# Rider products in blocks of three weight rows instead of two, in an expert layer that streams its weights

## The chip, the cores and the metric

One core of a Trainium2 chip runs the kernel. The metric is the device time of one execution, in microseconds (us). Three timed runs of the kernel before gave 2209.34, 2218.16 and 2219.35 us; the median is 2218.16. The profiled execution took 2214.47 us.

## The reference

One inference step of a two-layer encoder for 512 prompt tokens and 128 sample tokens (640 together), model width 1024, all in float32. Layer 0 ends in a dense SwiGLU, layer 1 in a mixture of eight experts with two per token. Only the experts matter here:

```
logits = x @ w_router + b_router; top_v, top_i = top_k(logits, 2); gates = softmax(top_v)
y = sum over e of comb[:, e] * ((silu(x @ we1[e]) * (x @ we3[e])) @ we2[e])
```

`we1[e]` and `we3[e]` are 1024 x 1408, `we2[e]` is 1408 x 1024.

## The kernel before

**Passes.** The expert layer runs in eleven passes, each with one expert's weights. A pass takes 128 tokens; in the first five (the "ridden" ones) 32 more tokens, the riders, go through the same weights. The up half of a pass multiplies by `we1` and `we3`, the down half by `we2`. The halves are staggered: up of pass 0, up of pass 1, down of pass 0, up of pass 2, down of pass 1 and so on. Three rounds of "down, then up" of ridden passes run in a loop; then come a ridden down, an up without riders, the last ridden down, and plain passes to the end.

**Weight rows.** Weights come as rows of 128 partitions: 16 up rows of 1408 columns (704 KB), called U0 to U15 here, and 11 down rows of 1024 columns (512 KB), D0 to D10. They go through a ring of nine places (`NPLACE`, line 76). SyncE issues one DMA per row (line 671) as soon as the place of the row nine earlier is free. The first TensorE instruction after a row's products and after what rides behind them frees the place: `free_place` (line 1575) lets it add one to `expert_used`.

**What happens to a row.** ScalarE makes a rounded copy ("upper", line 2303), VectorE subtracts it from the raw row and writes the rest ("lower", line 3192) over the raw row, in place. TensorE multiplies the 128 tokens by both parts: nine matmuls for an up row, six for a down row. The riders instead are multiplied by the raw row, in full float32, by `ride` (line 1632): four matmuls in four column groups of 32, each run as two passes. A ride waits until its row's DMA has landed (`expert_in`), and VectorE's subtraction waits for the ride (`rows_ridden`, line 3199), since it overwrites what the ride reads.

**Order on TensorE.** It is written out by hand and executed in order. With `LOOK` = 5, after the products of every second row c, TensorE rides rows c+5 and c+6. I call such a group of rides a block. In the up half blocks follow c = 1, 3, ..., 15; in the down half they follow f = 0, 2, ..., 10, and rows beyond D10 are the next half's U0 to U5. Between rows TensorE also turns (transposes) gathered tokens and products (`turn_rows`, `turn_riders`, `turn_product`, `turn_rider_product`).

**Other traffic.** GpSimd gathers the next tokens from HBM early in each down half and stores a pass's result, 512 KB and four times 32 KB, at the end of each down half, beside the weight rows.

Of the kernel before, what the change touches and what calls it, by code (L numbers as in the profile page):

```python
# [85 lines left out]
LOOK = 5  # L86
# [112 lines left out]
def build(nc, a, c, o, d):  # L199
# [11 lines left out]
    with ctx:  # L211
# [701 lines left out]
        def _(pe):  # L913
# [5 lines left out]
            def wait(s, value):  # L919
                pe.wait_ge(s, value)  # L920
# [4 lines left out]
            def claim(*banks):  # L925
                for b in banks:
                    if holder[b]:
                        wait(*holder[b])
                        holder[b] = None
# [17 lines left out]
            def product(out, x, y, first, last):  # L947

                ins = mm(out, x[0], y[0], first, False)
                mm(out, x[0], y[1], False, False)  # L950
                return ins, mm(out, x[1], y[0], False, last)
# [143 lines left out]
            for l in range(DEPTH):  # L1095
# [470 lines left out]
                if l % 2:  # L1566
# [8 lines left out]
                    def free_place(ins):  # L1575

                        if release[0]:
                            ins.then_inc(expert_used, 1)
                            release[0] = False

                    def weight_parts():

                        nonlocal place
                        take(expert_split)
                        at = place % NPLACE
                        place += 1
                        return expert_upper(at), ERL[:, at, :]

                    def turn_rows(half, bank):

                        if half == 0:
                            take(gathered_in, 16)
                        claim(bank)
                        for j in range(4):
                            ins = tr(PS[:, bank, tiles(j)], GR[:, tiles(4 * half + j)])
                            free_place(ins)
                        ins.then_inc(rows_turned, 1)
                        holder[bank] = (rows_split, n.add("rows_split"))
# [33 lines left out]
                    def ride(row, up_row=None, down_row=None):  # L1632

                        at = row % NPLACE
                        landed = 16 * (row // NPLACE + 1)
                        wait(expert_in[at], landed if riders.i is None else riders.i * (16 * PASS_ROWS // NPLACE) + landed)
                        if down_row is None:
                            k, which = UP_ORDER[up_row]
                            b, width, starts, first, last = 3 + 4 * which, RIDER_COLS, RIDER_AT, k == 0, k == KD - 1
                            stationary = [XR[:, k, :]] * 4  # L1640
                            if up_row == 0:
                                wait(riders_ready, riders.value("riders_ready"))
                        else:
                            b, width, starts, first, last = 2, D // 4, range(0, D, D // 4), down_row == 0, down_row == NF - 1
                            group, j = RIDER_BLOCK[down_row]
                            stationary = [ACTR[:, j, RIDERS * group:RIDERS * (group + 1)]] * 4
                            if down_row == 0:
                                wait(rider_product_ready, riders.value("rider_product_ready"))
                        if first:
                            claim(b)  # L1650
                        for g in range(4):
                            ins = mm(PS[RIDERS * g:RIDERS * (g + 1), b, 0:width], stationary[g],
                                     ER[:, at, starts[g]:starts[g] + width], first, last)
                        ins.then_inc(rows_ridden, 1)
                        if last:
                            made = {2: rider_y_ready, 3: rider_silu_made, 7: rider_product_made}[b]
                            holder[b] = (made, riders.add(made.name))

                    def up(ridden, following):

                        wait(rows_split, n.value("rows_split"))
                        for c in range(UP_ROWS):
                            k, which = UP_ORDER[c]
                            w = weight_parts()
                            for part in PART_ORDER:
                                first, end = PARTS[part]
                                b = 4 * which + part
                                if k == 0:
                                    claim(b)
                                begin, ins = product(PS[:, b, 0:end - first], [x[:, k, :] for x in (XGH, XGL)],  # L1670
                                                     [x[:, first:end] for x in w], k == 0, k == KD - 1)
                                free_place(begin)
                                if k == KD - 1:
                                    ins.then_inc((gates_summed, ups_summed)[which], 1)
                                    made = (silu_made, product_made)[which]
                                    holder[b] = (made, n.add(made.name))
                            release[0] = True
                            for ahead in range(c + LOOK, c + LOOK + 2) if c % 2 else ():
                                if ridden and ahead < UP_ROWS:
                                    ride(place - 1 + ahead - c, up_row=ahead)  # L1680
                                if following and UP_ROWS <= ahead < UP_ROWS + LOOK:
                                    ride(place - 1 + ahead - c, down_row=ahead - UP_ROWS)
                            if c == 13:
                                turn_rows(0, 0)

                    def down(ridden, rows, products):

                        banks = (0, 1) if ridden else (3, 7)
                        for f in range(NF):
                            w = weight_parts()  # L1690
                            if f == 0:
                                wait(product_split, n.value("product_split"))
                            for half, b in enumerate(banks):
                                if f == 0:
                                    claim(b)
                                begin, ins = product(PS[:, b, :], [x[:, f, :] for x in (ACTH, ACTL)],
                                                     [x[:, half * 512:(half + 1) * 512] for x in w], f == 0, f == NF - 1)
                                free_place(begin)
                                if f == NF - 1:
                                    ins.then_inc(down_summed, 1)  # L1700
                                    holder[b] = (moe_y_ready, n.add("moe_y_ready"))
                            release[0] = True
                            for ahead in range(f + LOOK, f + LOOK + 2) if f % 2 == 0 else ():
                                if ridden and ahead < NF:
                                    ride(place - 1 + ahead - f, down_row=ahead)
                                if rows == "ridden" and ahead >= NF:
                                    ride(place - 1 + ahead - f, up_row=ahead - NF)
                            if rows and f == 0:
                                turn_rows(1, 7 if ridden else 0)
                            if rows == "ridden" and f == 1:  # L1710
                                turn_riders(3)
                            if products and f in (4, 8):
                                turn_product(f // 4 - 1)
                            if products == "ridden" and f == 9:
                                turn_rider_product()
                        if products:
                            turn_product(2)
# [18 lines left out]
                    for c in range(LOOK + 1):  # L1736
                        ride(c, up_row=c)
                    up(True, False)
                    turn_rows(1, 1)
                    turn_riders(3)  # L1740
# [75 lines left out]
                for it in range(4):  # L1816
# [35 lines left out]
                    for j, blocks in enumerate(W2_CHUNKS):  # L1852
                        c = len(UP_CHUNKS) + j
# [1582 lines left out]
```

## Time and profile before

| | us |
|---|---|
| timed runs, median of 3 | 2218.16 (2209.34 to 2219.35) |
| profiled execution | 2214.47 |
| its span, first to last instruction | 2212.8 |
| expert layer, first row issued to last (DMA table) | 1496.7 to 2160.0 |
| rides, first to last | 1520.0 to 1905.4 |
| TensorE busy in the span | 2042.4 (92%) |
| VectorE busy | 1307.5 (59%) |
| ScalarE busy | 997.3 (45%) |

In the rows further down the first number is a start in us from the span's start, the next a duration; the text in square brackets is the time for which the engine was idle before, and what ended it. PE is TensorE, DVE VectorE, ACT ScalarE, POOL GpSimd, SPq the SyncE queue. All matmuls of the layer have line 941, since a helper records them; they are told apart by their tiles: `expert_ring,mix_t` is a ride of an up or down row (384 or 256 columns), `region_split`, `expert_lower` and `z_weights_upper` are products with the split rows. Lines 1889 and 2524 are the helpers of ScalarE and VectorE.

### The profile page before, as it was taken

The numbers are of one execution on the slowest core, as the hardware profiler recorded it, in microseconds if no ns is written. First come the engines' busy times: TensorE is split into PE (matmuls) and PEld (weight loads), VectorE is DVE, ScalarE is ACT, GpSimd is POOL, SyncE is SP. The second block draws the span as 40 slices with busy tenths as digits, with TensorE's granted clock in tenths as the row PEclk, the third lists the DMA queues.
The fourth block names the chain that finished last, engine by engine and source line by source line (L and its number), as shares of the span: only waits on it lengthen the run. The fifth ranks groups of instructions, "written<-read, shape, count | busy, mean of one in ns | idle before, by whom it ended". The sixth has DMA issues, their size and how long they took to land.

```text
span 2212.8 us, 36684 instructions
## 1 busy us (share of the span) xinstructions
PE 2042.4 (92%) x14292; PEld 1713.2 (77%) x14292; DVE 1307.5 (59%) x2052; ACT 997.3 (45%) x1456; POOL 185.1 (8%) x271
## 2 busy tenths in 40 slices
PE   6999868898999999998999788978999999999996
PEld 4999645588999999998998445866666667788883
DVE  3657654355544544456567643645566667789885
ACT  5422126444424433434221254434455556677782
POOL 3000120110000000000000011111010010011201
PEclk8999769998999999999998689978999999999998
DMA  9222669633545454642123266216677788899995
GB/s 319 77 77 77 164 185 300 206 103 96 169 127 167 129 159 127 166 146 78 60 77 86 58 222 207 83 61 228 224 260 248 256 279 324 323 372 375 371 385 190
DMA packets 272094, 418.23 MB, mean 189 GB/s; under 512 B 21214, under 2 KB 216312, under 8 KB 271952
## 3 DMA queue, kind: packets, MB, share of 16 engines
q1 hardware_dynamic: 249984, 349.50, 47.8%
q0 software_dynamic: 21968, 66.72, 9.2%
q8 instruction: 102, 1.67, 0.3%
q14 instruction: 40, 0.33, 0.0%
HBM read 385.73 MB, written 29.59 MB: 188 GB/s over the span
## 4 chain that ended last, share of the span: by engine, by line
PE 81%; DMA 6%; DVE 5%; ACT 3%; issue 2%; SPq 1%; ACTq 0%; POOL 0%; PEldq 0%; DVEq 0%; PEld 0%; POOLq 0%
PE banks L941 78%; PE banks L945 3%; DMA expert_ring<-in_we 2%; DMA weight_ring<-in_w_ada 2%; DVE scratch L2524 1%; ACT scratch L1889 1%; DVE region L2524 1%; ACT hidden_t L1889 1%; DMA scratch<-bias_rows 1%; SPq L588 1%; ACT region_split L1889 1%; ACTq L1904 0%; DMA mix_t<-h_rows,pass_tokens 0%; DMA weight_ring<-in_w_in 0%; DVE weights_lower L2524 0%
## 5 line engine op out<-in xcount | busy, mean ns | idle before, releaser
L941 PE MATMUL banks<-upper_parts,region_split 128*128 128x320 f32 x1664 | 390.5, 310 | 4.5 <-DVE upper_parts L2524 4.5
L941 PE MATMUL banks<-upper_parts,weights_lower 128*128 128x320 f32 (+1 forms) x1248 | 387.2, 310 | 0.0
L941 PE MATMUL banks<-region_split 128*128 128x320 f32 (+1 forms) x1264 | 338.9, 331 | 2.5 <-DVE upper_parts L2524 2.5
L2524 DVE TENSOR_TENSOR expert_lower<-expert_ring,region_split 128x1408 fp32r<-128x1408 f32 (+1 forms) x198 | 284.1, 1468 | 93.3 <-PE banks L941 64.0
L941 PEld LDWEIGHTS banks<-upper_parts,region_split 128*128 128x128 f32 x1664 | 284.9, 189 | 4.8 <-issue 4.8
L1889 ACT ACTIVATE region_split<-expert_ring 128x1408 fp32r<-128x1408 f32 (+1 forms) x198 | 242.3, 1256 | 68.8 <-DMA expert_ring<-in_we 56.4
L941 PEld LDWEIGHTS banks<-region_split 128*128 128x128 f32 x1264 | 222.9, 188 | 19.0 <-issue 4.8
L941 PEld LDWEIGHTS banks<-upper_parts,weights_lower 128*128 128x128 f32 (+1 forms) x1248 | 235.4, 189 | 0.0
L941 PE MATMUL banks<-region_split,upper_parts 128*128 128x384 f32 x732 | 226.5, 379 | 0.0
L2524 DVE TENSOR_TENSOR weights_lower<-weight_ring,region_split 128x2048 fp32r<-128x2048 f32 (+2 forms) x72 | 168.9, 2350 | 96.3 <-ACT region_split L1889 96.2
L1889 ACT ACTIVATE region_split<-weight_ring 128x2048 fp32r<-128x2048 f32 (+2 forms) x72 | 140.6, 1958 | 164.1 <-PE banks L941 162.5
L1889 ACT ACTIVATE region<-banks 128x320 f32<-128x320 f32 (+4 forms) x178 | 78.6, 461 | 267.4 <-PE banks L941 264.2
L941 PE MATMUL banks<-expert_lower,upper_parts 128*128 128x384 f32 x528 | 198.0, 375 | 0.0
L941 PE MATMUL banks<-z_weights_upper,upper_parts 128*128 128x256 f32 (+2 forms) x644 | 193.9, 335 | 0.6 <-ACT hidden_t L1889 0.5
L941 PE MATMUL banks<-region_split,weights_lower 128*128 128x320 f32 x608 | 187.9, 309 | 0.0
L2524 DVE TENSOR_TENSOR expert_lower<-expert_ring,z_weights_upper 128x1408 fp32r<-128x1408 f32 (+1 forms) x99 | 141.8, 1441 | 71.3 <-PE banks L941 45.6
L941 PE MATMUL banks<-upper_parts,z_weights_upper 128*128 128x320 f32 (+1 forms) x544 | 171.0, 314 | 11.7 <-DVE hidden_lower_parts L2524 10.2
L941 PE MATMUL banks<-hidden_lower_parts,z_weights_upper 128*128 128x320 f32 (+1 forms) x544 | 170.0, 313 | 0.0
L941 PEld LDWEIGHTS banks<-region_split,upper_parts 128*128 128x128 f32 x732 | 135.9, 188 | 32.1 <-issue 12.1
L1889 ACT ACTIVATE z_weights_upper<-expert_ring 128x1408 fp32r<-128x1408 f32 (+1 forms) x99 | 121.8, 1234 | 65.5 <-DMA expert_ring<-in_we 65.5
L941 PEld LDWEIGHTS banks<-z_weights_upper,upper_parts 128*128 128x128 f32 x644 | 120.9, 189 | 17.7 <-issue 7.6
L941 PEld LDWEIGHTS banks<-upper_parts,z_weights_upper 128*128 128x128 f32 (+1 forms) x544 | 102.9, 189 | 18.0 <-issue 15.6
(333 smaller groups left out, 3265.6 us busy)
## 6 DMA issues: line engine op xcount, KB each, us to landing
expert_ring<-in_we SPq DMA_DIRECT2D x176, 704.0 KB, 6.7
expert_ring<-in_we SPq DMA_DIRECT2D x121, 512.0 KB, 4.4
weight_ring<-in_w_ada SPq DMA_DIRECT2D x48, 1024.0 KB, 9.3
weight_ring<-in_w SPq DMA_DIRECT2D x88, 512.0 KB, 4.8
weight_ring<-in_w_in SPq DMA_DIRECT2D x24, 1024.0 KB, 5.2
weight_ring<-in_w SPq DMA_DIRECT2D x16, 1408.0 KB, 6.3
weight_ring<-in_w_out SPq DMA_DIRECT2D x8, 1024.0 KB, 7.0
y_rows<-residual_t POOLq DMA_DIRECT2D x4, 1760.0 KB, 23.6
```

Of the source, the lines that this page charges most:

```text
L588: sp.dma_start(dst, src).then_inc(weights_in[q % NSLOT], 16)
L941: return nc.tensor.matmul(out, lhsT, rhs, start=first, stop=last)
L945: return nc.tensor.transpose(out, in_, ident[0:k, 0:k])
L1889: return nc.scalar.activation(out, in_, f, **kw)
L2524: return v.tensor_tensor(out, x, y, op)
```

## The change

The blocks of rides become larger and rarer: three rows after every third row. In the up half they follow c = 1, 4, 7, 10, 13 and ride c+5, c+6 and c+7; in the down half they follow f = 0, 3, 6, 9 and ride f+5, f+6 and f+7. The same rides are made with the same operands; products, turns, frees and DMAs keep their order among themselves.

```
-                            for ahead in range(c + LOOK, c + LOOK + 2) if c % 2 else ():
+                            for ahead in range(c + LOOK, c + LOOK + 3) if c % 3 == 1 else ():
                                 if ridden and ahead < UP_ROWS:
                                     ride(place - 1 + ahead - c, up_row=ahead)
...
-                            for ahead in range(f + LOOK, f + LOOK + 2) if f % 2 == 0 else ():
+                            for ahead in range(f + LOOK, f + LOOK + 3) if f % 3 == 0 else ():
                                 if ridden and ahead < NF:
                                     ride(place - 1 + ahead - f, down_row=ahead)
```

## Rows read from the trace of the kernel before

**Rows 1.** The page: the span, and the chain that ended last by line
```profile
span 2212.8 us, 36684 instructions
...
PE banks L941 78%; PE banks L945 3%; DMA expert_ring<-in_we 2%; DMA weight_ring<-in_w_ada 2%; DVE scratch L2524 1%; ACT scratch L1889 1%; DVE region L2524 1%; ACT hidden_t L1889 1%; DMA scratch<-bias_rows 1%; SPq L588 1%; ACT region_split L1889 1%; ACTq L1904 0%; DMA mix_t<-h_rows,pass_tokens 0%; DMA weight_ring<-in_w_in 0%; DVE weights_lower L2524 0%
```
**Rows 2.** Busy time by stretch: ridden, then plain; last columns clock, DMA share, GB/s
```profile
1650.00:1700.00 50.00, 50.00 (x329) 33.85 (x328) 31.89 (x27) 27.72 (x28) 2.65 (x5) 1.00 0.76 256
...
2050.00:2100.00 50.00, 50.00 (x241) 42.45 (x240) 44.71 (x38) 39.24 (x40) 10.30 (x5) 1.00 0.97 380
```
**Rows 3.** PE in order of time: blocks after U1 and U3, first product between
```profile
1656.38 1.50 PE L941 MATMUL banks<-expert_ring,mix_t 128*32 128x384 f32 x16
1657.81 0.44 PE L941 MATMUL banks<-region_split,upper_parts 128*128 128x384 f32 x1
...
1661.84 1.50 PE L941 MATMUL banks<-expert_ring,mix_t 128*32 128x384 f32 x16
```
**Rows 4.** PE in order of time: blocks after D2 and D4 of the fourth down
```profile
1842.86 1.07 PE L941 MATMUL banks<-expert_ring,mix_t 128*32 128x256 f32 x16
...
1846.85 0.64 PE L941 MATMUL banks<-expert_ring,mix_t 128*32 128x256 f32 x8
1847.98 0.64 PE L941 MATMUL banks<-expert_ring,mix_t 128*32 128x256 f32 x8 [0.49 <-DMA expert_ring<-in_we]
```
**Rows 5.** Issues by SP: a U10, then U5, U8, U11, a later U8, a D10
```profile
1587.68 0.33 SPq L671 DMA_DIRECT2D expert_ring<-in_we  x1
...
1644.61 0.33 SPq L671 DMA_DIRECT2D expert_ring<-in_we  x1
...
1652.41 0.33 SPq L671 DMA_DIRECT2D expert_ring<-in_we  x1
...
1660.20 0.33 SPq L671 DMA_DIRECT2D expert_ring<-in_we  x1
...
1794.63 0.33 SPq L671 DMA_DIRECT2D expert_ring<-in_we  x1
...
1841.95 0.33 SPq L671 DMA_DIRECT2D expert_ring<-in_we  x1
```
**Rows 6.** ACT taking rows as they land: U10, then U2, U8, U11, a later U8
```profile
1591.67 1.38 ACT L1889 ACTIVATE z_weights_upper<-expert_ring 128x1408 fp32r<-128x1408 f32 x1 [1.94 <-DMA expert_ring<-in_we]
...
1643.49 1.39 ACT L1889 ACTIVATE region_split<-expert_ring 128x1408 fp32r<-128x1408 f32 x1 [0.35 <-DMA expert_ring<-in_we]
...
1660.00 1.38 ACT L1889 ACTIVATE z_weights_upper<-expert_ring 128x1408 fp32r<-128x1408 f32 x1 [3.21 <-DMA expert_ring<-in_we]
...
1665.42 1.38 ACT L1889 ACTIVATE region_split<-expert_ring 128x1408 fp32r<-128x1408 f32 x1 [0.43 <-DMA expert_ring<-in_we]
...
1801.46 1.38 ACT L1889 ACTIVATE z_weights_upper<-expert_ring 128x1408 fp32r<-128x1408 f32 x1 [2.46 <-DMA expert_ring<-in_we]
```
**Rows 7.** POOL: the store of a pass's result after D10
```profile
1652.05 0.60 POOL L854 DMA_DIRECT2D y_rows<-hidden_t  x1 [17.11 <-ACT hidden_t L1889]
```
**Rows 8.** PE: the block after D6, rides of U0 and U1
```profile
1640.45 0.85 PE L941 MATMUL banks<-expert_ring,mix_t 128*32 128x384 f32 x8
1641.78 0.85 PE L941 MATMUL banks<-expert_ring,mix_t 128*32 128x384 f32 x8 [0.48 <-DMA expert_ring<-in_we]
```
**Rows 9.** DMA issues of 1644.5 to 1644.8, U5: KB, us to landing
```profile
expert_ring<-in_we SPq DMA_DIRECT2D x1, 704.0 KB, 6.0
```
**Rows 10.** PE: second products of U10 and U11 (no riders), block after U11
```profile
1878.54 0.34 PE L941 MATMUL banks<-expert_lower,upper_parts 128*128 128x384 f32 x1
...
1880.45 0.34 PE L941 MATMUL banks<-expert_lower,upper_parts 128*128 128x384 f32 x1
...
1882.47 0.64 PE L941 MATMUL banks<-expert_ring,mix_t 128*32 128x256 f32 x8
1883.64 0.64 PE L941 MATMUL banks<-expert_ring,mix_t 128*32 128x256 f32 x8 [0.53 <-DMA expert_ring<-in_we]
```
**Rows 11.** PE: the longest wait in the ridden stretch
```profile
1578.53 2.48 PE L945 MATMUL banks<-ident,region 128*128 128x128 f32 x14 [3.88 <-DVE region L2524]
```
**Rows 12.** Busy time in the stretch behind that wait
```profile
1580.00:1585.00 5.00, 5.00 (x21) 4.45 (x20) 3.74 (x5) 4.83 (x6) 0.00 (x0) 0.69 0.01 3
```

More of the change, by code:

```diff
@@ L1677, in up @@
                             release[0] = True
-                            for ahead in range(c + LOOK, c + LOOK + 2) if c % 2 else ():
+                            for ahead in range(c + LOOK, c + LOOK + 3) if c % 3 == 1 else ():
                                 if ridden and ahead < UP_ROWS:
@@ L1702, in down @@
                             release[0] = True
-                            for ahead in range(f + LOOK, f + LOOK + 2) if f % 2 == 0 else ():
+                            for ahead in range(f + LOOK, f + LOOK + 3) if f % 3 == 0 else ():
                                 if ridden and ahead < NF:
```

## Prediction, written before the changed kernel had run

> **What bounds the kernel now.** I read the page first: four fifths of the chain that ended last are TensorE's own matmuls, 78% on line 941 [rows 1]. So in the expert layer nearly all that TensorE does or waits for moves the end. The view by stretches shows the same from another side: in the ridden stretch TensorE has work for all of 50 us, VectorE is busy for 31.9 us and the DMA share is 0.76; in the plain stretch the DMA share is 0.97 at 380 GB/s, but TensorE is again never idle [rows 2]. What a ridden pass loses is therefore not given back later. The clock is 1.00 in both, its 2.4 GHz level.
>
> Then I went through TensorE in order of time, for what a block costs, and through SyncE's issues and ScalarE's waits, for when rows land. ScalarE takes a row at once when it has been waiting for it, so its start is the landing time within some 0.03 us.
>
> **What the change removes: entries into blocks.** A ride leaves 8 records, and the first ride of a block, 8 records, ends 0.85 us after it began [rows 8]; two rides, 16 records, end after 1.50 [rows 3]. So a further up ride adds 0.65 us. For down rides it is 0.64 and 1.07, thus 0.43 [rows 4]. From one pair block to the next, with two up rows between, are 1661.84 - 1656.38 = 5.46 us [rows 3]. A row without a block takes 1880.45 - 1878.54 = 1.91 us [rows 10]. That leaves 5.46 - 2 x 1.91 - 2 x 0.65 = 0.34 us for entering and leaving a block; part of it is seen in the first product behind it, 0.44 us long [rows 3] where 0.33 to 0.34 is usual [rows 10]. In the down half the pair period is 1846.85 - 1842.86 = 3.99 [rows 4]; a down row, 6 matmuls of 512 columns against an up row's 4224 columns, is then 1.91 x 3072 / 4224 = 1.39, and the entry 3.99 - 2.78 - 0.86 = 0.35.
>
> The rides stay 135 in number, 12 of them ahead of the first two ups. Counted out from the code, blocks before: 5 and 8 in the first two ups, 6 + 8 in each of three loop rounds, 3 + 3 in the next down and up, 3 in the last ridden down: 64. After: 4 and 5, then 3 x (4 + 5), 2 + 2, 2: 42. The 22 entries saved give 22 x 0.34 = 7.5 us.
>
> **What it moves: each third row is ridden a row earlier.** This is the costly part. Row c+7 goes into the place of row c-2, which is freed when row c-1 begins. In the pair order row c+6 was the last of a block, freed one row sooner. So the time from freeing to riding the last row of a block falls by a whole row, to the rows c-1 and c, 3.82 us, and two rides, 1.3 us. From the DMA's issue, 0.37 to 0.5 us after the freeing, to the start of the third ride it is 2 x 1.91 - 0.37 + 0.10 + 0.35 + 3 x 0.32 = 4.9 us for an up row. TensorE executes in order: behind a ride that waits stand the next row's products, behind these the next frees, so SyncE's next issues and VectorE's subtractions come later too. Nothing of TensorE's can pass it, and the whole wait counts. Now each block:
>
> - U8, in the block after U1 (three loop rounds). It is issued at 1652.41, when TensorE turns the last product part, just after D10 [rows 5], at the very time at which the pass's result starts to be stored [rows 7]. It lands at 1660.00 [rows 6], 7.6 us later; now it is ridden only after U3. In the new block its ride could start at 1656.38 + 0.35 + 3 x 0.32 = 1657.7 [rows 3]: a wait of 2.4 us with the 0.09 us that PE takes after a landing. In the third round U8 takes 1801.46 - 1794.63 = 6.8 us [rows 5, 6]: a wait of 1.6. Taken: 3 x 2.0 = 5.9. Bounds: 0 and 7.5.
> - U11 and U14, in the blocks after U4 and U7 (five ups, ten cases). U11 was issued at 1660.20 and landed at 1665.42 [rows 5, 6], 5.2 us; wanted at 4.9, so a wait of 0.4. The least that a 704 KB row takes is 1591.67 - 1587.68 = 4.0 [rows 5, 6], no wait; a second row of a group tends to the slow side. Taken 0.35: 10 x 0.35 = 3.5. Bounds: 0 and 9, the latter at the 6 us of U5 [rows 9] less a little.
> - U5, in the block after D9 (three). Issued at D8's start, wanted after the rest of D8, the turn of a product part (0.4), D9 and two rides, some 4.1 us later. It takes 6.0 us now [rows 9] and 4.0 at the least: a wait of 0 to 2.0. With fewer DMAs ahead of it in the new order: 1.2, three times 3.6.
> - U1 and U2, in the block after D6 (three). Here TensorE waits already: U1's ride starts at 1641.78 where 1641.1 was possible, 0.7 us [rows 8]. U2, now ridden two rows later, lands at 1643.49 [rows 6] and is wanted at 1641.8: a wait of 1.7, which contains the old one. U0 and U2 are issued up to 1.4 and 1.0 us earlier in the new order, but two entries fewer bring the block nearer too. Additional wait -0.3 to 1.8, taken 0.8: 2.4.
> - D10, in the block after D3 (in the two downs that no ridden up follows). Issued at 1841.95 [rows 5], it lands so late that TensorE waits even after D4: from 1847.3 to 1847.98 [rows 4]. In the new order it is wanted at 1842.75 + 1.39 + 0.10 + 0.26 + 0.65 = 1845.2. The wait is 2.8 instead of 0.65, 2.2 more; two of them 4.4. With the low end, half of it, the gather that slows it would have to be over earlier.
> - D0 and D1, in the block after U10 of the up without riders. D0's ride starts at 1882.47 and D1's at 1883.64, the latter waiting [rows 10]; the new block would stand ready at 1880.45 - 0.17 + 0.10 = 1880.4 and can't be done before 1883.9. U11, 1.9 us, then comes behind it instead of before: 2.0 more.
> - Other blocks find their rows landed (D4 in the block after U13, D7 after D0, all rows of the first block): nothing.
>
> VectorE gets three rows to subtract at once, one after another; it has 18 us of 50 to spare in this stretch [rows 2], and the first row of a block is multiplied only four rows after it. That hides the bunching. Were that cover gone, a subtraction late would cost 1 to 2 us per block, some 40 to 80 us.
>
> Sum: 5.9 + 3.5 + 3.6 + 2.4 + 4.4 + 2.0 = 21.8 us of waits, less 7.5 us: 14.3 us more. On the profiled execution's 2214.5 that gives 2228.8; the median shown lies 3.7 us above it, so the forecast for a median is 2218.2 + 14.3 = 2232.5 us.
>
> A rule of the Trainium skill speaks for the change. "DMA: Bandwidth & Descriptors", in "Anatomy of one DMA", puts a DMA's time (fitted on GpSimd's path) at about 2.0 us plus bytes over 436 GB/s: for 720,896 bytes an estimate of 3.65 us. The trace does not agree where it matters: 4.0 at the least, 5.2 to 7.6 beside other transfers [rows 5, 6, 9]. By the rule all waits but those of D0 and D1 would be gone; it is the third rival below.
>
> **The rivals.**
> - The waits relieve each other (0.24). While TensorE waits it frees no places, so the DMA queues empty and the next row lands faster. Then U8 costs as above, but U11, U14, U5 and U2 next to nothing: 5.9 + 4.4 + 2.0 + 9.5 / 10 = 13.2, and if U8 too loses half of its wait, 10.3. Less 7.5 this is 3 to 6 us more, 2221 to 2224. For it: the DMA share of only 0.76 [rows 2] and 4.0 us for a row issued into calm [rows 5, 6]. Against it: U8's lateness has the result's store beside it [rows 7], which no wait of TensorE moves away.
> - On the other side (0.10): rows land in time because load sets the landing, and the new order spreads it. One mechanism: at the 4.0 us of the quiet U10 [rows 5, 6] a row beats each of the distances 4.1 (U5), 4.9 (U11, U14) and 5.3 (U8). It decides from the point at which U8 lands within 5.3 us of its issue. Then only the 22 entries are left, -7.5 us, 2210.7; with D0 and D1 still late 2212.7. Rows of 5.2 to 7.6 us speak against it. By the page's 3.65 us it would come out at the same 2210.7 to 2212.7.
> - The waits cost the clock (0.06). After TensorE had waited 3.88 us [rows 11] the next 5 us were granted 0.69 [rows 12], which is partly the 1.2 GHz level. The waits here are up to 2.8 us (D10) and 2.4 us (U8). If each of these five dropped the clock as there, (1 - 0.69) x 5 = 1.6 us each, 8 us would come on top: 2240. Against it: the waits of 0.5 to 1 us in the ridden stretch are followed by no drop [rows 2].
>
> **How the numbers follow.** Forecast 0.60, the others 0.24, 0.10 and 0.06. A measurement of this kernel can tell about 0.5%, 11 us, from no change: under 2207 counts as faster, over 2229 as slower. The forecast's own range is 2225 to 2240. The whole range begins at 2212, where the waits just pay for themselves less the scatter of the runs, and ends at 2245, with the upper bounds 7.5, 9, 6, 5.4, 4.4 and 2.0 (34.3 less 7.5 is 26.8 more). Slower: 0.62, from the forecast without its lower edge and from the clock case. Within: 0.33, from that edge, the first rival and most of the second. Faster: 0.05, half of the second rival.
>
> **What would show it.** TensorE's waits for `expert_ring` DMAs between 1520 and 1905 should rise from about 3 us to over 20, the largest behind U1, D3 and, once, U10; U8's ride should start right after ScalarE's start on U8. The pair period of 5.46 us should become 3 x 1.91 + 6 rides' passes of 0.32 + 0.34 = 8.0 us for three rows where nothing waits. The plain stretch should be as long as before. I am wrong if U8 lands within 5.3 us of its issue, if a block's entry costs far more or less than 0.34 us, or if VectorE's subtractions become what products wait for.

## The result, and the profile after

| | before | after |
|---|---|---|
| median (lowest to highest) | 2218.22 us (2209.34 to 2219.35), 6 runs | 2241.45 us (2234.45 to 2244.41), 6 runs |
| ratio | | 1.0103, 95% interval 1.0087 to 1.0119 |
| profiled execution | 2214.47 | 2243.98 |
| first to last issue of an expert row | 1496.7 to 2160.0: 663.3 us | 1502.7 to 2189.4: 686.7 us |

The kernel is 23 us slower. In the profiled executions 6.0 of the 29.5 us of difference lie before the first expert row, in code that did not change; over the executions profiled for this case that start lies anywhere from 1496.0 to 1503.3. So I compare the length of the expert layer, issue to issue: 23.4 us longer. One run of e11, an experiment below, took 6708.4 us, three times as long as any other; it is left out of every figure here.

The page after, span and chain; against [rows 1] TensorE's share of the chain falls from 78% to 76% and that of the expert rows' DMAs rises from 2% to 5%:

```profile
span 2242.3 us, 36684 instructions
...
PE banks L941 76%; DMA expert_ring<-in_we 5%; PE banks L945 4%; DVE scratch L2524 1%; ACT scratch L1889 1%; DVE region L2524 1%; ACT hidden_t L1889 1%; DMA scratch<-bias_rows 1%; ACT region_split L1889 1%; ACT region L1889 0%; ACTq L1904 0%
```

TensorE's waits for expert rows (total us, times, longest), before, then after:

```profile
PE banks L941 <- DMA expert_ring<-in_we: 3.6, 7, 0.7
```
```profile
PE banks L941 <- DMA expert_ring<-in_we: 24.4, 20, 4.9
```

Busy time by stretch, after (the columns are those of [rows 2]: length, busy time of TensorE, its weight loads, VectorE, ScalarE and GpSimd, then clock, DMA share and GB/s). The first two lines are the ridden stretch, the last the plain one [rows 2]. In the ridden stretch TensorE now idles and the clock is no longer 1.00; the plain stretch is as it was.

```profile
1600.00:1650.00 50.00, 48.11 (x332) 32.71 (x330) 30.05 (x27) 24.49 (x27) 2.37 (x4) 1.00 0.75 243
1650.00:1700.00 50.00, 46.45 (x285) 31.91 (x285) 27.84 (x22) 26.51 (x27) 2.65 (x5) 0.97 0.73 243
...
2050.00:2100.00 50.00, 50.00 (x241) 42.46 (x240) 43.73 (x37) 38.54 (x38) 3.81 (x4) 1.00 0.98 382
```

TensorE in order of time, after, from the block behind D9 to the block behind U7 of the first loop round; x24 is the number of records in a group, 8 for each ride:

```profile
1656.11 1.50 PE L941 MATMUL banks<-expert_ring,mix_t 128*32 128x384 f32 x16
1659.60 0.85 PE L941 MATMUL banks<-expert_ring,mix_t 128*32 128x384 f32 x8 [1.99 <-DMA expert_ring<-in_we]
1660.38 0.90 PE L945 MATMUL banks<-ident,region 128*128 128x128 f32 x3
1660.93 0.78 PE L941 MATMUL banks<-z_weights_upper,region_split 128*128 128x512 f32 x1
1661.51 0.63 PE L941 MATMUL banks<-expert_lower,region_split 128*128 128x512 f32 x1
...
1667.97 2.14 PE L941 MATMUL banks<-expert_ring,mix_t 128*32 128x384 f32 x24
1670.04 0.45 PE L941 MATMUL banks<-region_split,upper_parts 128*128 128x384 f32 x1
...
1675.98 1.50 PE L941 MATMUL banks<-expert_ring,mix_t 128*32 128x384 f32 x16
1678.33 0.85 PE L941 MATMUL banks<-expert_ring,mix_t 128*32 128x384 f32 x8 [0.84 <-DMA expert_ring<-in_we]
...
1685.04 0.53 PE L941 MATMUL banks<-expert_ring,mix_t 128*32 128x384 f32 x4
```

Three things are to be seen. Where the third row has landed, a block is one group of 24 records in 2.14 us (behind U1: no wait for U8 here). Where it has not, the group breaks into 16 and 8 with the wait between: 2.0 us for U5, 0.8 us for U11. And behind the wait for U5 a matmul of 512 columns takes 0.63 us instead of 0.39: part of D10's products ran at the 1.2 GHz level. From the block at 1675.98 to the next are 9.06 us; less the wait that is 8.0 to 8.2, where [rows 3] had 5.46 for two rows.

The granted clock around the three places in the ridden part where this happened, and at a fourth near the layer's end (second number from the end but one):

```profile
1660.00:1665.00 5.00, 5.00 (x25) 3.90 (x18) 0.00 (x0) 2.21 (x4) 0.00 (x0) 0.66 0.42 149
...
1900.00:1910.00 10.00, 8.96 (x51) 6.62 (x55) 4.91 (x4) 3.57 (x4) 0.00 (x0) 0.83 0.55 173
1928.00:1938.00 10.00, 8.91 (x38) 6.67 (x39) 3.29 (x3) 4.21 (x5) 0.00 (x0) 0.73 0.61 190
...
2184.00:2194.00 10.00, 9.44 (x34) 7.64 (x35) 7.32 (x7) 5.86 (x7) 0.54 (x1) 0.83 0.67 232
```

Not every such wait was followed by a fall. Around the wait for U5 of the third loop round (2.17 us, until 1808.34) and around the first of the waits for D10 shown below (2.30 us, until 1865.83) the clock stayed at 1.00:

```profile
1806.00:1816.00 10.00, 7.83 (x54) 5.49 (x54) 4.30 (x3) 6.00 (x8) 2.64 (x5) 1.00 0.75 266
1864.00:1874.00 10.00, 8.17 (x44) 6.39 (x45) 6.11 (x7) 4.33 (x5) 0.00 (x0) 1.00 0.83 289
```

And the two waits for D10 in the block behind D3, after (for before, see [rows 4]):

```profile
1865.83 0.64 PE L941 MATMUL banks<-expert_ring,mix_t 128*32 128x256 f32 x8 [2.30 <-DMA expert_ring<-in_we]
...
1929.09 1.08 PE L941 MATMUL banks<-expert_ring,mix_t 128*32 128x256 f32 x8 [4.90 <-DMA expert_ring<-in_we]
```

### The profile page after: what moved, and what is told of

Its sections match the earlier page's. It is cut to its first block, busy times and chain, and to the rows that moved or that the text cites. A ratio compares the mean times of both kernels' runs of the same rounds, so it can differ in the third digit from the quotient of the medians.

```text
span 2242.3 us, 36684 instructions
## 1 busy us (share of the span) xinstructions
PE 2051.8 (92%) x14292; PEld 1723.7 (77%) x14292; DVE 1305.9 (58%) x2052; ACT 996.3 (44%) x1456; POOL 175.6 (8%) x271
## 3 DMA queue, kind: packets, MB, share of 16 engines
q8 instruction: 102, 1.67, 0.3%
## 4 chain that ended last, share of the span: by engine, by line
PE 80%; DMA 8%; DVE 5%; ACT 4%; issue 2%; ACTq 0%; POOL 0%; PEldq 0%; DVEq 0%; PEld 0%; POOLq 0%; SPq 0%
PE banks L941 76%; DMA expert_ring<-in_we 5%; PE banks L945 4%; DVE scratch L2524 1%; ACT scratch L1889 1%; DVE region L2524 1%; ACT hidden_t L1889 1%; DMA scratch<-bias_rows 1%; ACT region_split L1889 1%; ACT region L1889 0%; ACTq L1904 0%; DVE weights_lower L2524 0%; DMA hidden_t<-h_rows,pass_tokens 0%; DMA weight_ring<-in_w_ada 0%; ACT L1889 0%
```

## The experiments

Theory A is the prediction's: the last row of a block of three is ridden one row sooner after its place is freed, and TensorE waits for its landing. Theory B, a rival: three rides in a row cost by themselves, because VectorE gets its rows in bunches. Theory C, the prediction's last rival made a second cause: the waits lower the clock. "Layer" is first to last issue of an expert row in the profiled execution, against 663.3 us before. "PE waits for rows" is TensorE's time in waits for rows from 1536 to 1935, and how often. All ratios are against the kernel before on the same chip: its median was 2216.8 us beside e1 to e4, 2217.1 beside e5 to e8 and 2217.6 beside e9 to e12.

| label | blocks | LOOK | median | ratio (95%) | layer | PE waits for rows |
|---|---|---|---|---|---|---|
| before | 2 and 2 | 5 | 2218.2 | 1 | 663.3 | 3.6 us, 7 times |
| after | 3 and 3 | 5 | 2241.5 | 1.0103 (1.0087 to 1.0119) | +23.4 | 24.4, 20 |
| e1 | up 3, down 2 | 5 | 2234.5 | 1.0082 (1.0052 to 1.0112) | +16.9 | 17.5, 15 |
| e2 | up 2, down 3 | 5 | 2235.3 | 1.0067 (1.0039 to 1.0095) | +18.4 | 17.0, 12 |
| e3 | 3 and 3 | 4 | 2209.0 | 0.9969 (0.9950 to 0.9988) | -7.7 | 1.8, 2 |
| e4 | 2 and 2 | 4 | 2215.0 | 0.9987 (0.9971 to 1.0002) | -1.6 | none |
| e5 | 4 and 4 | 3 | 2205.9 | 0.9940 (0.9918 to 0.9962) | -10.0 | 1.8, 3 |
| e6 | 3 and 3 | 3 | 2206.6 | 0.9940 (0.9921 to 0.9959) | -10.5 | none |
| e7 | 1 and 1 | 5 | 2237.0 | 1.0084 (1.0059 to 1.0109) | +17.9 | 2.8, 3 |
| e8 | e1 with filling | 5 | 2229.0 | 1.0056 (1.0035 to 1.0077) | +11.6 | 10.1, 16 |
| e9 | e6 again | 3 | 2209.2 | 0.9953 (0.9936 to 0.9970) | -9.0 | none |
| e10 | e5 again | 3 | 2207.0 | 0.9954 (0.9937 to 0.9970) | -10.7 | 1.4, 1 |
| e11 | e1 again | 5 | 2231.0 | 1.0060 (1.0040 to 1.0080) | +11.2 | 16.2, 19 |
| e12 | e8 again | 5 | 2228.2 | 1.0049 (1.0031 to 1.0067) | +15.2 | 11.5, 14 |

**e1 and e2: each half of the change alone.** e1 takes only the line of the up half from the change, e2 only that of the down half.

> Blocks of three in the up halves only, pairs in the down halves. Theory A (the last row of a block is ridden one row sooner after its place is freed, and TensorE waits for its landing): 14 entries less, -4.8 us; U8 is again issued beside the result's store and late, since no wait for U5 stands ahead of it: 3 x 2.0; U11 and U14 0.2 to 1.0 each as in the changed kernel, together about 4.5; D0 and D1 2.0. Sum about +7 to +8 us, ratio 1.003 to 1.004. Theory B (three rides in a row cost by themselves, by bunching VectorE's subtractions): the loss of 21 us goes by blocks, 14 of 22 of it: +13 us. Theory C (the clock falls after long waits): no fall here, as no wait reaches 3 us.

> Blocks of three in the down halves only. Theory A: 8 entries less, -2.8 us; waits for U2 (1.0 more in each loop round), U5 (1.7 to 2.4 in each), D7 about 0.8 once, D10 2.2 and about 4.4: together +15, sum about +12 us, ratio 1.0055. Theory B: 8 of 22 of 21 us, +8 us. Theory C: D10's product after the wait for U5 runs at half clock in at least one round, 1 us each, within the +12.

Both halves lose, and both more than expected: +18 us for +7 to +8 in e1, +15 to +18 for +12 in e2. Their sum is more than the whole change (layers +16.9 and +18.4 against +23.4, ratios +0.82% and +0.67% against +1.03%), so they share something. A part of it is U8. TensorE in e1, the block behind U1 of the first loop round, the product behind it, and ScalarE's take of the same row:

```profile
1656.99 1.50 PE L941 MATMUL banks<-expert_ring,mix_t 128*32 128x384 f32 x16
1660.92 1.30 PE L941 MATMUL banks<-expert_ring,mix_t 128*32 128x384 f32 x8 [2.44 <-DMA expert_ring<-in_we]
1662.15 0.69 PE L941 MATMUL banks<-region_split,upper_parts 128*128 128x384 f32 x1
```
```profile
1660.90 1.38 ACT L1889 ACTIVATE z_weights_upper<-expert_ring 128x1408 fp32r<-128x1408 f32 x1 [3.52 <-DMA expert_ring<-in_we]
```

The ride starts within 0.02 us of ScalarE's take of the same row: it is the landing that ends the wait. From where the third ride could start (1656.99 + 0.35 + 3 x 0.32 = 1658.3) it is 2.6 us, and the other two rounds have 2.6 and 2.45: 7.7 us for U8 where the prediction had 5.9, and where the whole change has 2.3. There the wait for U5 stands just ahead, the DMA share is down to 0.42 when U8 is issued (the row 1660.00:1665.00 above), and in round one U8 lands in time (the unbroken group at 1667.97 above). e1 was expected at +7 to +8 and came at +18 (its repeat e11 at +13): theory A's sum fell short. Besides the larger waits for U8, and one of 2.55 us for the last D10 though e1's down halves are unchanged, the clock was missing from it. The matmul at 0.69 us shows it, and so does the clock in the stretches behind the three waits for U8, 0.91 over 20 us each, 1.8 us of clock apiece:

```profile
1600.00:1660.00 60.00, 57.71 (x392) 38.99 (x390) 36.93 (x34) 32.10 (x36) 5.85 (x9) 1.00 0.79 265
1660.00:1680.00 20.00, 18.31 (x110) 12.13 (x110) 9.23 (x7) 10.64 (x11) 0.00 (x0) 0.91 0.66 223
1735.00:1755.00 20.00, 18.44 (x111) 12.06 (x112) 9.40 (x7) 10.16 (x11) 0.00 (x0) 0.91 0.68 228
1810.00:1830.00 20.00, 19.37 (x115) 13.50 (x116) 9.43 (x7) 10.97 (x11) 0.00 (x0) 0.91 0.65 220
```

So the expectation of no fall in e1, since no wait reaches 3 us, was wrong. In e2 the clock fell behind two of the three waits for U5 (1.96 and 2.11 us) and both for D10 (3.36 and 3.56 us), 0.83 over the 10 us around each.

Theory B would have e1 lose nearly twice what e2 does, by blocks; they lose the same within their intervals. Taken alone, e1's loss is nearer to B's +13 us than to A's +7 to +8, and e11's +13 is B's figure. So these two runs don't decide; the next does.

**e3 and e4: the same blocks, ridden later after the freeing.**

```
-LOOK = 5
+LOOK = 4
```

(e3: with both lines of the change; e4: with pairs.)

> The change with LOOK = 4: after every third row the rows c+4, c+5 and c+6 are ridden, so the last row of a block has the same distance from its freeing as in the kernel before, and the first rows are ridden a row later than there. Theory A: the added waits go, the 22 entries stay saved: -7.5 us against before, or a little better where the old waits for U1, D0, D1 and D10 shrink; ratio 0.996 to 0.997. Theory B: still 21 us slower than before, or more, as VectorE has one row less between ride and product; ratio 1.01.

> The kernel before with LOOK = 4: pairs of rows c+4 and c+5. The last row of a block is ridden a row later after its freeing than before. Theory A: the old waits of TensorE on expert rows, about 4.5 us, mostly go, entries stay: -3 to -4 us, ratio 0.998; against it the three-row kernel with LOOK = 4 is 3 to 5 us faster. Theory B: no different from before, unless VectorE becomes late, then slower.

This decides between A and B. e3 has exactly the changed kernel's blocks and makes it some 30 us faster than the change (0.9969 against 1.0103), and faster than before with an interval clear of 1, as theory A gave it. By theory B it had to stay slow. TensorE in e3, three blocks of the first up in the loop, all unbroken:

```profile
1656.55 2.14 PE L941 MATMUL banks<-expert_ring,mix_t 128*32 128x384 f32 x24
...
1664.56 2.14 PE L941 MATMUL banks<-expert_ring,mix_t 128*32 128x384 f32 x24
...
1672.59 2.14 PE L941 MATMUL banks<-expert_ring,mix_t 128*32 128x384 f32 x24
```

e4 removes the old waits and gains at most a little: its interval touches 1. (In its profiled execution, as in those of e9 and after, the layer's last stretch ran at 0.83 over 10 us behind a wait for VectorE, which costs it as much as 2 us of layer.)

**e5 and e6, and again as e10 and e9: LOOK = 3.** e5 rides four rows after every fourth (`range(c + LOOK, c + LOOK + 4) if c % 4 == 1`, and `f % 4 == 0`), e6 is the change with LOOK = 3.

> LOOK = 3 and blocks of four, after every fourth row: rows c+3 to c+6. The last row of a block keeps the distance of the kernel before, and there are 33 blocks instead of 64: 31 entries saved, -10.5 us. Theory A: about 10 us faster than before, 3 us faster than three rows with LOOK = 4, ratio 0.995. Theory B (bunching makes VectorE late): the first row of a block has only two rows between ride and product, 3.8 us for a landing on VectorE of 1.6 us, but D3 is now ridden only after the next half begins, and VectorE's multiplications wait for it; if that shows, the gain is smaller than 7 us or a loss.

> LOOK = 3 and blocks of three: rows c+3 to c+5, the last row one row later after its freeing than before. Theory A: entries -7.5 us, the old waits on expert rows (4.5 us) gone: -11 to -12 us, ratio 0.995, unless VectorE becomes late. Theory B: slower than LOOK = 4 with three, since VectorE has one row less.

> LOOK = 3 with blocks of three, once more and with more rounds: is it faster than LOOK = 4 with three (7 us) and equal to LOOK = 3 with four? Theory A: 22 entries of 0.33 us and the old waits, -9 to -12 us, ratio 0.9950, interval below 0.998.

> LOOK = 3 with blocks of four, once more: 9 more entries saved than with three, 3 us, but in the three loop rounds U3 is waited for, 0.4 to 1.6 us each. Theory A: equal to the kernel with three within 1.5 us, ratio 0.9945 to 0.9955.

Both are 0.5 to 0.6% faster than before in both measurements, 9 to 11 us by the layer, and equal to each other: four rows save three more microseconds of entries and wait 1.8 us for U3 and 0.8 us for ScalarE instead (e5). In e6 TensorE has no wait for a row from 1536 to 1935. No matmul there waits for a subtraction in either. But TensorE's weight loads (PEld), which overlap matmuls, do in e5, and not in e6. In total us, times and the longest, e5:

```profile
PEld banks L941 <- DVE expert_lower L2524: 9.4, 15, 0.6
```

So with four rows and LOOK = 3 VectorE is only just in time. These two kernels are the best versions found.

**e7: one ride after every row**, row c+6 after row c, 123 blocks instead of 64:

```
-                            for ahead in range(c + LOOK, c + LOOK + 2) if c % 2 else ():
+                            for ahead in (c + LOOK + 1,):
...
-                                if following and UP_ROWS <= ahead < UP_ROWS + LOOK:
+                                if following and UP_ROWS <= ahead < UP_ROWS + LOOK + 1:
...
-                            for ahead in range(f + LOOK, f + LOOK + 2) if f % 2 == 0 else ():
+                            for ahead in (f + LOOK + 1,):
```

> One ride after every row: row c+6 after row c, the same distance from freeing to the last (here only) ride less one ride. 123 blocks instead of 64. It measures the entry: with 0.34 us each 59 x 0.34 = +20 us, less up to 4 us of old waits that the slower rows cover: +16 to +20 us, ratio 1.008. If entries cost nothing and only the distance counts, as theory B would have it for large blocks, it is equal to before or faster.

It measures the entry. TensorE in e7, then in e5, blocks of one and of four in an up half:

```profile
1668.24 0.85 PE L941 MATMUL banks<-expert_ring,mix_t 128*32 128x384 f32 x8
...
1671.13 0.85 PE L941 MATMUL banks<-expert_ring,mix_t 128*32 128x384 f32 x8
```
```profile
1662.75 2.79 PE L941 MATMUL banks<-expert_ring,mix_t 128*32 128x384 f32 x32
...
1673.32 2.79 PE L941 MATMUL banks<-expert_ring,mix_t 128*32 128x384 f32 x32
```

The periods are 2.89 us for one row, 5.46 for two [rows 3], 8.01 for three (e3) and 10.57 for four. Less 1.91 and 0.65 us for each row, 0.33, 0.34, 0.33 and 0.33 us are left: the entry costs the same whatever the size of the block.

**e8, and again as e12: the wait filled with work.** e1 with `FILLS` = 10 matmuls of 512 columns in bf16, whose output nothing uses, ahead of U8's ride in the loop rounds:

```
+                                if ridden and ahead == 8 and riders.i is not None:
+                                    claim(4)
+                                    fill(4, FILLS)
```

> Blocks of three in the up halves only (as in the first experiment), and in the three loop rounds 10 filling matmuls of 512 columns in bf16 on a free bank, some 2.2 us, right before U8's ride, so that TensorE works while it would wait 2.6 us. Their output is used by nothing. Theory C (waits of this length cost a stretch at half clock, 1.7 us each): the three half-clock stretches behind U8 go, -5 us against the first experiment, about +13 us against before; the waits themselves stay. If the clock does not depend on the wait, or costs nothing, the time is that of the first experiment, +17 to +18 us.

> Blocks of three in the up halves only, again, beside the kernel with filling matmuls on the same chip. Theories A and C together: +17 us, ratio 1.0075.

> The same with 10 filling matmuls before U8's ride in the three loop rounds; their output is used by nothing. Theory C: 5 to 6 us faster than the kernel without them, run on the same chip, +11 to +12 against before, and no half-clock stretch behind U8. Without theory C: no difference between the two.

TensorE in e8, first loop round (the products have line 942 here):

```profile
1656.20 1.50 PE L942 MATMUL banks<-expert_ring,mix_t 128*32 128x384 f32 x16
1657.63 2.33 PE L942 MATMUL banks<-spread,ident 128*128 128x512 bf16 x10
1659.95 0.85 PE L942 MATMUL banks<-expert_ring,mix_t 128*32 128x384 f32 x8
1660.73 0.44 PE L942 MATMUL banks<-region_split,upper_parts 128*128 128x384 f32 x1
```

The ride of U8 starts as late as in e1, about 3.8 us behind the block's first, but takes 0.85 us instead of 1.30, and the product behind it 0.44 instead of 0.69. Over the 300 us from 1600 to 1900 the granted clock is 1.00 in e8 where e1 has 0.97 (e1, then e8):

```profile
1600.00:1900.00 300.00, 286.33 (x1814) 200.74 (x1813) 185.75 (x155) 163.45 (x169) 21.70 (x35) 0.97 0.76 261
```
```profile
1600.00:1900.00 300.00, 292.70 (x1891) 202.32 (x1890) 187.09 (x157) 163.88 (x170) 21.70 (x35) 1.00 0.79 265
```

The repeat is less plain: there the granted clock is 0.99 over these 300 us in both kernels. Behind U8's ride it fell in three of three rounds in e1 and in one of three in e11, and in none of six with filling. In e11 it stayed at full speed behind a wait of 1.36 us and, in the third round, behind one of 2.87:

```profile
1811.32 0.85 PE L941 MATMUL banks<-expert_ring,mix_t 128*32 128x384 f32 x8 [2.87 <-DMA expert_ring<-in_we]
1812.11 0.44 PE L941 MATMUL banks<-region_split,upper_parts 128*128 128x384 f32 x1
```

e12 has its slow products behind other waits, that for D10 (1.96 us, until 1865.06) and that for D0 (2.20 us). Of the 15 waits of 1.9 us and more for rows in after, e1, e2 and e11, 11 were followed by a fall and 4 were not (2.17 and 2.30 us in after, 2.55 in e1, 2.87 in e11). What decides between them was not settled.

So work in the wait's place kept the clock behind U8, six times of six. The price in time is less sure. e8's median is 5.5 us below e1's, run on another chip; e12's is 2.7 us below e11's on the same chip, where 5 to 6 was expected. The intervals of the ratios overlap in both pairs, and the profiled layers go 5.3 us down in the first and 4.0 us up in the second. Theory C's mechanism was seen; that it costs some 1.7 us a fall is read from the clock, not from the medians.

## Why the prediction was right, and where its terms were off

The sign and the range held: 2241.45 lies in 2212 to 2245 and outside the forecast's own range, 2225 to 2240. The forecast was +14.3 us, the measured +23. That the whole range held is partly luck: its upper end was added up from upper bounds of waits alone, and 6 of the 9 us by which the forecast fell short are clock (2 of them scatter, as said below), for which it had no term. The terms after sum to 22.8 of the layer's 23.4 us. Waits are read from the starts of rides, less those of before (so U5's first wait is 2.2 us here, where the row above shows 1.99 idle):

| term | forecast | after |
|---|---|---|
| entries, 22 x 0.34 | -7.5 | -7.5 (0.33 to 0.34 each, e3, e5, e7) |
| U8, 3 cases | 5.9 | 0 + 0.65 + 1.67 = 2.3 |
| U11 and U14, 10 cases | 3.5 | 4.7 |
| U5, 3 cases | 3.6 | 2.2 + 1.7 + 2.3 = 6.2 |
| U1 and U2, added, 3 rounds | 2.4 | 2.8 |
| D10, added, 2 cases | 4.4 | 6.3 |
| D0 and D1 | 2.0 | 2.0 idle, 1.4 more than before |
| D7, D4 | 0 | 1.0 |
| a wait for ScalarE at 1859.6 before, gone | 0 | -0.5 |
| clock | 0 (a rival) | about 4 in the ridden part, 2 at the end |

The clock's 4 us are the sum of what matmuls between which no ride or wait stands took longer than the same ones before: 1.35 us around 1660, 1.35 around 1905 and 1.37 around 1930.

- **Entries removed**: right in size, and e3 shows them as a gain.
- **Each third row ridden a row earlier**: right as a mechanism; e1 to e6 bear it out from both sides.
- **U8** was oversized, because it was priced alone. Alone, in e1, it cost 7.7 us. In the whole change the wait for U5 just ahead lets the transfers drain. This much of the first rival ("the waits relieve each other") was right, but only here. In one of three rounds U8 even landed within 5.3 us of its issue (1664.04, ridden at 1669.28), which the prediction had named as a sign of being wrong; in the other two it took 5.9 and 6.9. The largest waits stood behind D3 and D9, not behind U1.
- **U5** was undersized: the 1.2 us assumed that fewer DMAs ahead would speed it up. It landed 5.7 to 6.35 us after its issue, as slow as before [rows 9].
- **D10**, the second case: its wait was 5.1 us, not 2.8. It landed 8.2 us after issue where before it was 5.8. e1, whose down halves are unchanged, had some 8.0 there as well. In e11, the same kernel as e1, it landed 6.6 us after issue, so a good part is scatter between executions. The row goes with the gather that GpSimd issues 0.6 us ahead of it: that took 6.6 us before, 9.0 after, 8.8 in e1 and 7.4 in e11. Which delays which was not tried.
- **The clock** was given 0.06 as a rival that adds to the forecast. It was a term of the sum. The price was right (1.6 us a fall); the chance, and the 0 in the sum, were not. The chance was judged from one example, a wait of 3.88 us [rows 11], and from waits of 0.5 to 1 us that cost nothing. After, the clock fell behind a wait of 2.0 us. Nor was that example the only one in the trace before: behind an idle 0.56 us, ahead of the first rides of the second pass (1568.87), the clock was 0.72 over 1570 to 1575.
- **VectorE hides the bunching**: right. For what room is left, see e5.
- **The second rival**, rows landing in time in the new order, fell: 20 waits. The quickest row of 704 KB in the trace after (a U10, issued at 1594.99) landed 3.9 us after its issue. That is more than the 3.65 us estimated from the Trainium skill's "DMA: Bandwidth & Descriptors", "Anatomy of one DMA".
- **The plain stretch is as before**: right, but for the slow stretch at 2184 to 2194. It follows a wait of 2.4 us for VectorE (1.5 before), 250 us after the last ride. e4 and e9, in which no ride waits, have such a stretch there too, behind 2.3 and 1.8 us. I count it, like the 6 us ahead of the layer, as scatter between executions.

## What to carry to other kernels

Grouping work on TensorE saves a fixed price per group (here 0.34 us for each switch to the 32-column rides and back), but the last member of a larger group is wanted earlier relative to the freeing of its buffer; work out that lead for every place of the loop and compare it with the slowest landing there, not the median. Here the cure was one constant: with LOOK = 4 or 3 the same blocks turned +1.0% into -0.3% and -0.5 to -0.6%. Price waits in one queue together, for one relieves the next, and give every wait of some 2 us on TensorE a good chance (11 of 15 here) of a stretch at half clock behind it.

## What was unexpected of the hardware

- Waits of 2.0 us (after) and 2.4 us (e1) on TensorE were followed by matmuls of 512 and 384 columns at 0.63 and 0.69 us instead of 0.39 and 0.44, and by a granted clock of 0.66 over 5 us (after); behind waits of 2.17 to 2.87 us in after, e1 and e11 it stayed at 1.00 four times. With ten bf16 matmuls in the wait's place it did not fall in six of six rounds (e8, e12).
- A weight row of 704 KB landed 3.9 us after issue at the least and up to 8.3 us beside a 512 KB store (the third round's U8 in e11, at a DMA share of 0.83 over 1803.0 to 1811.3, where 1600 to 1900 had 0.78). One of 512 KB took up to 8.2 us beside a gather (the last ridden D10, after).
- The price of an entry, 0.33 to 0.34 us, did not depend on whether one, two, three or four rides follow (e7, before, e3, e5).
